# Two transformer blocks in one kernel: router weights in a buffer of their own, and a first expert turn that gathers only its own two experts

## What is computed

```python
def _hierarchical_moe(x, w_rg, b_rg, w_re, b_re, w_gate, w_up, w_down):
    g_logits = (xf @ w_rg + b_rg)                                   # 4 groups
    g_w, g_idx = lax.top_k(jax.nn.softmax(g_logits, axis=-1), 1)
    e_logits = (xf @ w_re + b_re).reshape(t, 4, 8)                  # 8 experts per group
    e_logits = e_logits[jnp.arange(t), g_idx[:, 0]]
    e_w, e_idx = lax.top_k(jax.nn.softmax(e_logits, axis=-1), 2)
    e_w = e_w / jnp.sum(e_w, -1, keepdims=True)
    gates = (g_w * e_w)
    ...
    h = jax.nn.silu(xb @ w_gate[e]) * (xb @ w_up[e])                # 1024 -> 512
    return h @ w_down[e]                                            # 512 -> 1024
```

## Time and profile before

| | us |
|---|---|
| median of 3 runs | 2864.51 (2863.2 to 2865.44) |
| profiled execution, its own time | 2863.64 |
| its span, first to last instruction | 2861.6 |
| TensorE busy | 2665.7 (93%) |
| VectorE busy | 1282.7 (45%) |
| ScalarE busy | 1029.2 (36%) |
| GpSimd busy | 69.0 (2%) |
| DMA | 695.32 MB, mean 243 GB/s |

### The profile page before, as it was taken

How to read it: one execution, slowest core, us unless ns; L and a number is a source line. 1 busy time by engine, 2 the same in 40 slices (tenths; PEclk the granted TensorE clock), 3 DMA queues, 4 the chain that set the end, 5 groups by cost and what they waited for, 6 DMA issues and landing times.

```text
span 2861.6 us, 40274 instructions
## 1 busy us (share of the span) xinstructions
PE 2665.7 (93%) x16540; PEld 1958.4 (68%) x16540; DVE 1282.7 (45%) x2346; ACT 1029.2 (36%) x1629; POOL 69.0 (2%) x28
## 2 busy tenths in 40 slices
PE   8999999999999999999989989989988999998996
PEld 7988888899898988889888744333336864333333
DVE  5565554755656565565678641111116653111112
ACT  4444563444444465344457531111114442111111
POOL 0001000100100100010010000000000000000000
PEclk9999999999999999999999999999999999999999
DMA  9636643565463843456353379999996219999996
GB/s 307 214 111 160 211 100 127 172 206 177 162 206 102 243 144 92 162 167 201 119 164 119 100 272 422 421 421 422 421 417 202 89 49 421 421 422 421 421 421 290
DMA packets 313986, 695.32 MB, mean 243 GB/s; under 512 B 57104, under 2 KB 242320, under 8 KB 264656
## 3 DMA queue, kind: packets, MB, share of 16 engines
q1 hardware_dynamic: 310896, 682.24, 65.1%
q10 hardware_dynamic: 2912, 10.52, 1.2%
HBM read 691.63 MB, written 1.08 MB: 242 GB/s over the span
## 4 chain that ended last, share of the span: by engine, by line
PE 62%; DMA 21%; DVE 10%; ACT 5%; issue 2%; SPq 0%; ACTq 0%; DVEq 0%
PE ps L282 25%; DMA ring<-in_moe_w_gate 20%; PE ps L790 7%; PE ps L2518 7%; PE ps L1533 3%; PE ps L1573 3%; DVE weight_parts L223 3%; PE ps L313 3%; PE ps L2535 2%; PE ps L2568 2%; PE ps L294 2%; ACT weight_parts L215 1%; PE ps L2456 1%; PE ps L1460 1%; DVE tiny L906 1%
## 5 line engine op out<-in xcount | busy, mean ns | idle before, releaser
L282 PE MATMUL ps<-xT_upper,weight_parts 128*128 128x256 f32 (+1 forms) x4656 | 851.8, 285 | 25.1 <-DVE xT_lower L932 11.3
L223 DVE TENSOR_TENSOR weight_parts<-ring,weight_parts 128x1024 fp32r<-128x1024 f32 x479 | 612.3, 1281 | 502.1 <-ACT weight_parts L215 501.7
L282 PEld LDWEIGHTS ps<-xT_upper,weight_parts 128*128 128x128 f32 (+1 forms) x4656 | 722.4, 190 | 50.2 <-issue 19.4
L215 ACT ACTIVATE weight_parts<-ring 128x1024 fp32r<-128x1024 f32 x479 | 503.9, 1055 | 544.2 <-PE ps L282 326.3
L282 PE MATMUL ps<-xT_lower,weight_parts 128*128 128x256 f32 (+1 forms) x2328 | 658.1, 283 | 0.0
L282 PEld LDWEIGHTS ps<-xT_lower,weight_parts 128*128 128x128 f32 (+1 forms) x2328 | 441.4, 190 | 0.2
L2518 PE MATMUL ps<-ring,bias_tiles 128*64 128x512 f32 x1024 | 240.2, 596 | 33.7 <-DMA ring<-in_moe_w_gate 17.9
L2518 PE MATMUL ps<-ring,arena 128*64 128x512 f32 x1024 | 240.4, 596 | 33.0 <-DMA ring<-in_moe_w_gate 17.2
L2807 DVE TENSOR_TENSOR bias_tiles<-ps,bias_tiles 128x512 f32<-128x512 f32 x32 | 22.1, 692 | 503.5 <-ACT bias_tiles L2664 503.5
L2568 PE MATMUL ps<-moe_slots,bias_tiles 128*64 128x512 f32 x1024 | 229.2, 596 | 4.4 <-ACT bias_tiles L2667 4.4
L790 PE MATMUL ps<-weight_parts,hidden_upper 128*128 128x512 f32 x704 | 218.4, 391 | 1.7 <-DVE hidden_lower L842 1.7
(11 more groups left out here) (325 smaller groups left out, 2847.9 us busy)
## 6 DMA issues: line engine op xcount, KB each, us to landing
ring<-in_ffn_w SPq DMA_DIRECT2D x132, 1024.0 KB, 5.2
ring<-in_moe_w_up SPq DMA_DIRECT2D x128, 1024.0 KB, 24.3
ring<-in_moe_w_gate SPq DMA_DIRECT2D x128, 1024.0 KB, 24.4
moe_slots<-in_moe_w_down SPq DMA_DIRECT2D x128, 1024.0 KB, 20.2
ring<-in_w_gate SPq DMA_DIRECT2D x24, 1024.0 KB, 7.6
ring<-in_w_in SPq DMA_DIRECT2D x20, 1024.0 KB, 7.2
ring<-in_ssd_w_in SPq DMA_DIRECT2D x20, 1024.0 KB, 5.4
ring<-in_attn_w_qkv SPq DMA_DIRECT2D x18, 1024.0 KB, 9.6
```

What stands on the lines that cost most here:

```text
L215: act.activation(self.part(n, 0), cut(self.stream.slot(pos)), ACT.Copy).then_inc(self.upper_done, 1)
L223: dve.tensor_tensor(self.part(n, 1), cut(self.stream.slot(pos)), self.part(n, 0).bitcast(F32), ALU.subtract).then_inc(self.split, 1)
L282: m = pe.matmul(out[0:rows, :], w[of_w][:, k, :], c.xTp[of_x][:, k, :], start=(k == 0 and (of_w, of_x) == PARTS[0]), stop=(k == KT - 1 and ...
```

## The change

- The router weights get a buffer of their own, `router_weights`. The first layer's load is issued at the end of the program's set-up, the second layer's in the first MoE stage behind its first-turn slots. The MoE turns begin at ring slot 0 without the router in slot 7.
- Their split is in the norm in front: ScalarE copies between its two `normed`, VectorE subtracts between its two `raw`. The parts lie in memory of the weight units, which is free by then. The router's products start behind the first `x_parts`; a `keep_clock` of 1024 columns ahead of them and one of 512 ahead of the gather are gone.
- The first gather is split by columns: experts 0 and 1 (128 columns) ahead of turn 0, experts 2 and 3 in turn 0 behind `hidden(0)`, where the four transposes of the tables now stand too. The first `choose` of the turns follows the hidden product.
- Lower rows of the second tokens are made by GpSimd. One count product with an all-zero block is left out; in VectorE's chain a copy is saved, two additions become one, and the group's subtraction moves behind the mask.

```diff
@@ setup_stage, SyncE
         s.issue(sp, RING)
+        load_router(c, sp, 0)
@@ norm_stage, VectorE
             raw(0)
...
+            if router:
+                dve.wait_ge(R.hi.sem, R.hi.at(1))
+                dve.tensor_tensor(c.router_parts[1], c.router_w[:, :], c.router_parts[0].bitcast(F32), ALU.subtract).then_inc(R.split.sem, R.split.one())
             raw(1)
@@ norm_stage, ScalarE, between normed(0) and normed(1)
+            if router:
+                act.wait_ge(c.units.done, c.units.limit)
+                act.wait_ge(R.landed.sem, R.landed.issued)
+                act.activation(c.router_parts[0], c.router_w[:, :], ACT.Copy).then_inc(R.hi.sem, R.hi.one())
@@ MoePlan
-        s.align(RING - 1)
-        self.router = s.direct(...)
+        s.align(0)
@@ moe_programs, SyncE
             s.issue(sp, p0 + TURN)
+            if l + 1 < DEPTH:
+                sp.wait_ge(R.split.sem, R.split.at(0))
+                load_router(c, sp, l + 1)
@@ moe_programs, TensorE
-            keep_clock(c, pe, CLOCK_ROUTER[0], 0)
-            pe.wait_ge(R.split.sem, R.split.at(1))
+            pe.wait_ge(R.split.sem, R.split.at(0))
...
-                for u in range(TT):
+                for u in range(t + 1):
...
             keep_clock(c, pe, CLOCK_ROUTER[2])
+            gather(0, 0, TURN_COLS[0])
             pe.wait_ge(c.aux_dve.sem, c.aux_dve.at(5))
             pe.transpose(ps[0:1, MOST, 0:P], most[:, 0:1], c.ident[:, :]).then_inc(c.aux_pe.sem, c.aux_pe.one())
-            keep_clock(c, pe, CLOCK_ROUTER[3])
-            gather(0, 0)
-            pe.wait_ge(c.aux_dve.sem, c.aux_dve.at(4))
-            gather(0, 1)
+            gather(0, 1, TURN_COLS[0])
...
                     hidden(i)
                     if i:
                         scatter(i - 1)
+                    else:
+                        turned()
+                        for half in range(2):
+                            gather(0, half, TURN_COLS[1])
                     transpose_hidden(i)
@@ moe_programs, ScalarE, behind Silu of turn 0
+                    if i == 0:
+                        tokens_out(0, 0, TURN_COLS[1])
+                        tokens_out(0, 1, TURN_COLS[1])
@@ moe_programs
+        @block.gpsimd
+        def _(pool):
+            lower_rows(pool, 1)
@@ moe_programs, VectorE
-            dve.tensor_tensor(eg, lg[:, :, 0:4], over(sc[:, 0, :], 1, 4), ALU.subtract).then_inc(c.aux_dve.sem, c.aux_dve.one())
...
-            do(dve.tensor_copy(sc[:, 3, :], sc[:, 0, :]))
...
             dve.tensor_tensor(sc[:, 5, :], sc[:, 0, :], sc[:, 3, :], ALU.subtract).then_inc(c.aux_dve.sem, c.aux_dve.one())
+            dve.tensor_tensor(eg, lg[:, :, 0:4], over(sc[:, 4, :], 1, 4), ALU.subtract).then_inc(c.aux_dve.sem, c.aux_dve.one())
...
-            lower_rows(1)
```

More of the change, by code:

```diff
@@ L858, in norm_loader, with norm_stage @@
     return load
-def norm_stage(c, weight, done, last=False, lead=(), upto=0):
+def norm_stage(c, weight, done, last=False, lead=(), upto=0, router=False):
     nc, ps, block = c.nc, c.ps, c.block
@@ L882, in half @@
         return v[:, 4 * h:4 * h + 4, t * P:(t + 1) * P]
+    R = c.router
+    if router:
+        flat = c.units.parts.rearrange("p u w n -> p (u w n)")
+        c.router_parts = [flat[:, w * KT * 36:(w + 1) * KT * 36] for w in range(2)]
     @block.sync
@@ L2296, in every, with load_router @@
     return v[:, first:first + step * (P - 1) + 1:step]
+def load_router(c, sp, l):
+    w = c.router_w.rearrange("p (k n) -> p k n", k=KT)
+    for name, lo, hi in (("moe_w_router_group_2", 0, 4), ("moe_w_router_expert_2", 4, 36)):
+        sp.dma_start(w[:, :, lo:hi], c.a[name][l].rearrange("(k p) n -> p k n", p=P)).then_inc(c.router.landed.sem, 16)
+    c.router.landed.issued += 32
 class MoePlan:
@@ L2363, in rtake @@
         return v
-    w_router = [rtake(KT * 36).rearrange("p (k n) -> p k n", k=KT) for _ in range(2)]
+    rtake(2 * KT * 36)
+    w_router = [part.rearrange("p (k n) -> p k n", k=KT) for part in c.router_parts]
     x_parts = [rtake(2 * D).rearrange("p (t n) -> p t n", t=2) for _ in range(2)]
@@ L2443, in _, with gather @@
         def _(pe):
-            def gather(m, half):
+            def gather(m, half, cols=slice(0, 2 * PAIR)):
                 pe.wait_ge(K.chosen, m + 1)
-                if m == 0:
+                if m == 0 and cols.start == 0:
                     pe.wait_ge(c.x_split.sem, c.x_split.at(2))
+                    pe.wait_ge(c.aux_dve.sem, c.aux_dve.at(4))
+                elif m == 0:
+                    pe.wait_ge(K.xe, half + 1)
                 else:
-                    pe.wait_ge(K.xe, 2 * m + half)
+                    pe.wait_ge(K.xe, 2 * m + half + 2)
                 o = gathered_banks(m, half).rearrange("p b (k n) -> p (b k) n", k=2)
@@ L2635, in _, with tokens_out @@
         def _(act):
-            def tokens_out(m, half):
-                act.wait_ge(K.gathered, 2 * m + half + 1)
-                act.activation(xe[m % 2][:, 4 * half:4 * half + 4, :], gathered_banks(m, half).rearrange("p b (k n) -> p (b k) n", k=2), ACT.Copy
+            def tokens_out(m, half, cols=slice(0, 2 * PAIR)):
+                act.wait_ge(K.gathered, half + 1 + (0 if m == 0 and cols.start == 0 else 2 * m + 2))
+                act.activation(xe[m % 2][:, 4 * half:4 * half + 4, cols], gathered_banks(m, half).rearrange("p b (k n) -> p (b k) n", k=2)[:, :, cols], ACT.Copy
                                ).then_inc(K.xe, 1)
-            s.ready(act, plan.router)
-            act.activation(w_router[0], cols8(s.slot(plan.router))[:, :, 0:36], ACT.Copy).then_inc(R.hi.sem, R.hi.one())
             act.wait_ge(R.ps.sem, R.ps.at(1))
@@ L2728, in _ @@
             dve.wait_ge(c.x_parts.sem, c.x_parts.at(0))
-            dve.wait_ge(R.hi.sem, R.hi.at(1))
-            dve.tensor_tensor(w_router[1], cols8(s.slot(plan.router))[:, :, 0:36], w_router[0].bitcast(F32), ALU.subtract).then_inc(R.split.sem, R.split.one())
-            dve.wait_ge(R.split.sem, R.split.at(1))
-            dve.sem_inc(s.used, 1)
             dve.tensor_tensor(picks[0:64, :], c.ident[0:64, 0:32], c.ident[0:64, 32:64], ALU.add)
```

87 lines of the change are left out of this document (45 added, 42 removed).

## The result

The changed kernel takes **2879.67 us** (median of 5 runs, 2877.38 to 2880.07), the kernel before on the same chip 2864.25 (5 runs): ratio 1.0054, 95% interval 1.0043 to 1.0065. That is 15.4 us slower, where 2863.7 had been forecast and the range ended at 2867.5. The profiled execution took 2877.38 us, with a span of 2875.2: 13.6 above the span before.

A forecast was written before the change was run, and what follows sets the result against it. Each MoE stage was taken to end when its weight stream, at 421 GB/s, ends. First stage: 1.55 us gained less 0.7 given back, 0.85; second stage: 0; median 2864.51 - 0.85 = 2863.7 us, range 2859.8 to 2867.5.

The forecast's parts named there:

- Step 1: Router weights' split moved into the norm: VectorE's chain starts 1.0 us earlier, the router's other 2 us are slack.
- The unseen: Chance of 0.08 kept for something not foreseen anywhere in the kernel, faster or slower.
- Step 5: First gather narrowed to 128 columns: 4.0 us in all, so hidden(0) starts 1.55 us earlier.
- could come back: 1.1: First gather: TensorE pauses as long before it as before, so the low clock could return and cost 1.1 us.
- The other estimate for the pace: First gather: a sustained 81 ns per narrow product instead of 111, making the gather 1.0 us shorter.
- Step 3: Second tokens' lower rows on GpSimd: its instruction takes 3.0 us and holds VectorE up, 2.6 us lost (2.0 to 3.7).
- The estimate from the Trainium skill: GpSimd's lower rows at about twice VectorE's time: 4.0 us instead of 3.0, the sum 1.0 us worse.
- Steps 1, 2 and 4: Ahead of the first gather: chain starts 1.0 us earlier, fewer small instructions save 0.4, gather begins 0.7 earlier.
- Step 6: Turn 0 takes on transposes and the gather for experts 2 and 3: down(0) 6.7 us after hidden(0), 0.7 given back.
- The second stage: Second MoE stage: bound by its weight stream, gains 0; TensorE's first turn can be about 1 us later without loss.
- the worst case: Whole kernel: GpSimd at 4.1 us, low clock in gather and turn, 2.7 lost in the first stage, 1.7 in the second: 2868.0.
- narrow rounded products lose their fast pace: Rival, both gathers: 215 ns per narrow product, 5.5 us lost in the first stage, 4.5 in the second: 2874.5, chance 0.08.

The follow-up runs named there:

- e4: The changed kernel with the first gather 256 columns wide in front again and nothing of it in turn 0: 2871.56 us, ratio 1.0024.
- e3: The changed kernel with the lower rows of the second tokens back on VectorE, GpSimd doing nothing: 2877.54 us, ratio 1.0051.
- e7: The changed kernel with 32 unused words behind the router weights, the wide front gather and 5632 columns of zeros ahead of the counts: 2861.74 us, ratio 0.9992.
- e5: The changed kernel with 32 unused words behind the router weights and 5632 instead of 2560 columns of zeros ahead of the counts: 2865.58 us, ratio 1.0008.

## Why the prediction was wrong

- **What was not in the sum at all.** The sum has no term for the new buffer itself. Step 1 put the router weights "in a buffer of their own" and costed their loads and their split, right as far as it went; what the buffer does to all that lies behind it was not asked. It was 5.6 us before the first MoE (6.1 in the feed-forward layers), the largest part of the loss. "The unseen" had 0.08, on either side.
- **Step 5 failed.** It took 111 ns per narrow product and 0.3 us for a remainder at the low clock, 4.0 us in all. The 111 ns were right, at full clock: turn 0 shows 110. The clock was wrong: the gather took 7.1 us with all of it at 0.50, and so was the start of hidden(0), which took 1.0 us longer in the first stage and 2.4 in the second. The working even named the low clock as something that "could come back: 1.1". It took the clock for a matter of the pause ahead alone. The narrow products, which were to bring the gain, ran under the low clock to their end where the wide ones of e4, behind the same pause, were out of it after about 2 us. That the width itself is worth little was costed rightly (111 against 118 ns). Of the 0.85 us that the step won (5.1 against 4.0 and 0.25), about 0.4 were the transposes moved to the turn, 0.2 the width, and 0.4 a low clock taken to be mostly gone; the transpose of the maximum took 0.15 back.
- **The other estimate for the pace** would have erred further: by the sustained 81 ns of the Trainium skill (TensorE: Matmul & The Clock Gate, Back-to-back issue gap) the gather was to be 1.0 us shorter still. This case's 32-bit rounded products of 128 columns stand 110 ns apart at full clock and 217 at half (the mean over the first 16).
- **Step 3 right, its remark apart.** GpSimd's instruction took 2.85 us (forecast 3.0, bounds 2.4 to 4.1), and VectorE stood still for it: 2.76 instead of 0.23, so 2.5 lost (2.6 forecast). The estimate from the Trainium skill (GPSIMD Engine Reference, section 4.1), 4.0, is refuted by the 2.85. What I missed: whom the wait holds. TensorE's pause ahead of the counts grew from 0.84 to 5.35 us. GpSimd's instruction made 2.5 of that (without it, e3 has 2.85); the other 2.0 come from step 1: TensorE's router products and the zeros behind them end 3.4 us earlier, the chain that it waits for only about 1.4. What the step called slack became a longer pause.
- **Steps 1, 2 and 4 right.** From the norm's first instruction, the chain's first (L2784) stands at 19.35 us against 20.46, 1.1 earlier (1.0 forecast). The gather started 29.86 behind it against 30.87, 1.0 earlier (0.7).
- **Step 6 about right, and small.** From hidden(0)'s end to down(0) it took 7.1 us (1708.68 to 1715.77), forecast 6.7. The wide kernel at full clock takes 4.7 (e7, without the narrow gather in the turn), so the work moved into the turn costs 2.4; the 6.0 of the kernel before held some low clock.
- **The second stage was 0 in the sum**, with 1 us of slack. The slack exists but is smaller: with down(0) 4.5 us later than before, 60.43 behind the norm's instruction against 55.90, the stage ends 4.15 later; in e3 3.9 us cost 3.5, in e5 2.2 cost 1.4. That is 0.4 to 0.7 us of slack. The error is step 5's, felt twice.
- **A slip in the worst case.** 2868.0 adds the losses to the profiled execution; added to the median, as the forecast is, they give 2868.9. The stated range left both out, and the measured 2879.67 lies beyond either.
- **The rival that ended on the other side** was "narrow rounded products lose their fast pace", 215 ns in both gathers, 2874.5 us, chance 0.08. In the front gather its number came true (217 ns), by another mechanism, the clock; in turn 0 it did not hold. Its price for the first stage, 5.5, was too high (3.1), that for the second, 4.5, near (4.15).

## What to carry to other kernels

A new buffer is a change to every product whose operands lie on different sides of it: compare two kernels at the same distances modulo 256 bytes, and try the eight steps of 32 bytes once, since 8 unused words gave this tuned kernel 0.65%. Before narrowing products to save columns, see at which granted clock they will run: here the narrowed ones sat at half clock for 7 us, and the wide ones did not. Price a wait by every engine that stands behind it, TensorE's clock among them.

## What the runs showed of the hardware

- Products of 128x128 by 256 columns in the rounded 32-bit type take 117.8 ns (11.31 us for 96) to 120 ns (11.52) by the distance of their operands modulo 256 bytes; measured at 0, 32, 64, 96, 160 and 192. Products of 512 columns moved too (24 in 5.44 to 5.49 us) with their own operands at a fixed distance.
- The granted clock fell from 1.00 to 0.50 in the middle of the narrow gather with TensorE busy throughout (e5, between 1683 and 1684, the last pause being 1.35 us ahead of 1680.89). In turn 0, behind hidden(0), 32 products of the same shape ran at full clock, 110 ns each, and the clock stayed at 1.00. What tells the two apart is not shown.
- Halving the width hardly shortened a product: 110 ns for 128 columns and 120 for 256 between starts at the granted clock 1.00, and 213 for both at 0.50 (the narrow gather of the changed kernel; the start of the wide gather of the kernel before).
- VectorE's small instruction stretched to GpSimd's length again, 2.76 beside 2.85 us.
